# The first stage of a decoder layer: the first two weight blocks multiplied side by side, slice by slice

## The reference, cut to what matters

```python
mod = jax.nn.silu(c) @ w_ada + b_ada
sh1, sc1, gt1, sh2, sc2, gt2 = jnp.split(mod[:, None, :], 6, axis=-1)
u = x * (1 + sc1) + sh1
proj = u @ w_in
xa, ga, q, k, v = jnp.split(proj, [D_A, 2 * D_A, ...], axis=-1)
y_a, new_conv, h_last = rglru_branch(xa, ga, ...)
```

## Time and profile before

| | us |
|---|---|
| median of three runs | 1359.38 |
| lowest and highest of them | 1357.69, 1365.87 |
| span of the profiled execution, first to last instruction | 1363.8 |
| PE busy in it | 1196.5 (88%) |
| ACT busy, DVE busy | 577.3, 735.4 |

### The profile page before, as it was taken

How to read it: one execution, slowest core, us unless ns; L and a number is a source line. 1 busy time by engine, 2 the same in 40 slices (tenths; PEclk the granted TensorE clock), 3 DMA queues, 4 the chain that set the end, 5 groups by cost and what they waited for, 6 DMA issues and landing times. The chain is left out here.

```text
span 1363.8 us, 20897 instructions
## 1 busy us (share of the span) xinstructions
PE 1196.5 (88%) x6933; PEld 907.3 (67%) x6934; DVE 735.4 (54%) x1247; ACT 577.3 (42%) x845; POOL 137.3 (10%) x129
## 2 busy tenths in 40 slices
PE   5699899999699979969995389999999999999854
PEld 3699787877255647627783277777778877778721
DVE  3356534343356747527545775789641455476147
ACT  2556443111245644214233264677531454465124
POOL 0000000000000001002431200011000000000055
PEclk8799899999699999879997599999999999999977
DMA  9985931259669948877333596899661455597184
GB/s 333 368 289 195 354 126 64 70 179 333 242 206 352 307 134 273 272 208 233 126 119 130 183 335 261 324 380 399 232 234 62 138 215 210 214 371 268 38 342 178
DMA packets 102028, 316.94 MB, mean 232 GB/s; under 512 B 12845, under 2 KB 21533, under 8 KB 95290
## 3 DMA queue, kind: packets, MB, share of 16 engines
q1 hardware_dynamic: 85146, 273.97, 57.5%
q0 software_dynamic: 6432, 23.33, 4.8%
q10 hardware_dynamic: 10384, 18.76, 3.7%
HBM read 281.22 MB, written 101.93 MB: 281 GB/s over the span
## 5 line engine op out<-in xcount | busy, mean ns | idle before, releaser
L2584 DVE TENSOR_TENSOR e_downl<-e_wd,e_downh 128x1024 fp32r<-128x1024 f32 x64 | 74.1, 1220 | 65.3 <-ACT e_downh L2479 65.3
L2646 PE MATMUL e_psY<-e_downh,e_hTh 128*128 128x512 f32 x216 | 91.0, 421 | 15.7 <-DVE e_hTl L2605 14.5
L2479 ACT CAST e_downh<-e_wd 128x1024 fp32r<-128x1024 f32 x64 | 62.4, 1048 | 68.5 <-DMA e_wd<-in_w_exp_down 68.5
L552 PE MATMUL n_psA<-n_wh,u_h 128*128 128x512 f32 (+1 forms) x216 | 88.1, 408 | 0.4 <-DVE n_wl L811 0.4
L2646 PE MATMUL e_psG<-e_gateh,e_xTh 128*128 128x512 f32 x216 | 86.4, 400 | 2.0 <-DVE e_gatel L2578 2.0
L2646 PE MATMUL e_psG<-e_uph,e_xTh 128*128 128x512 f32 x216 | 87.8, 406 | 0.2 <-issue 0.2
L2648 PE MATMUL e_psG<-e_gatel,e_xTh 128*128 128x512 f32 x216 | 85.9, 398 | 0.0
L2647 PE MATMUL e_psG<-e_gateh,e_xTl 128*128 128x512 f32 x216 | 85.9, 398 | 0.0
L554 PE MATMUL n_psA<-n_wh,u_l 128*128 128x512 f32 (+1 forms) x216 | 85.8, 397 | 0.0
L2647 PE MATMUL e_psY<-e_downh,e_hTl 128*128 128x512 f32 x216 | 85.7, 397 | 0.0
L2648 PE MATMUL e_psY<-e_downl,e_hTh 128*128 128x512 f32 x216 | 85.5, 396 | 0.0
(11 more groups left out here) (406 smaller groups left out, 2573.0 us busy)
## 6 DMA issues: line engine op xcount, KB each, us to landing
e_wg<-in_w_exp_gate SPq DMA_DIRECT2D x16, 2048.0 KB
e_wu<-in_w_exp_up SPq DMA_DIRECT2D x16, 2048.0 KB
e_wd<-in_w_exp_down SPq DMA_DIRECT2D x16, 2048.0 KB, 14.4
out_k_s<-in_cache_win_k SPq DMA_DIRECT2D x8, 4088.0 KB, 21.1
out_v_s<-in_cache_win_v SPq DMA_DIRECT2D x8, 4088.0 KB, 34.5
a_wring<-in_w_ada SPq DMA_DIRECT2D x16, 1024.0 KB, 5.3
scratch_y<-e_y ACTq DMA_DIRECT2D x54, 256.0 KB, 4.3
n_wr<-in_w_in SPq DMA_DIRECT2D x20, 512.0 KB, 7.0
```

Of the source, the lines that this page charges most:

```text
L552: nc.tensor.matmul(dst, lh, rh, start=(k == 0), stop=False)
L2479: nc.scalar.copy(w["down"][H_][:, k, :], ew["down"][:, k, :]).then_inc(s_dh.sem, s_dh.unit)
L2584: nc.vector.tensor_tensor(w["down"][L_][:, k, :], ew["down"][:, k, :], w["down"][H_][:, k, :], ALU.subtract).then_inc(s_dl.sem, s_dl.unit)
L2646: nc.tensor.matmul(dst, left[H_], right[H_], start=first, stop=False)
```

## The change

SP issues the bias and the last three slices of `w_ada` of half 0 ahead of pieces 0 and 1. On PE, `branch` loses its range of k, and a new function `first_branches(k, halves)` multiplies slice k with X0 and with G0 one after the other; G0 takes the pair with the lower u second and that with the lower weight last. It waits for the upper and lower parts separately, ahead of each group of three matmuls. The eight slices of modulation half 1 are spread: four before the products of k = 0, and the rest between the products of k = 0, 1 and 2. `turn_mod(1)` follows k = 2. On ACT the order becomes `scaled(k)`, `upper_u(k)` for each k, with the cast of piece 1 after k = 0. On DVE `lower(0)` moves behind the modulation of the sample tokens and `lower(1)` behind `lower_u(0)`. In the ACT and DVE loops the condition k == 0 holds in half 0 only.

```diff
--- before.py
+++ after.py
@@ -388,15 +388,15 @@
             for k in range(3, 5):
                 load_ada(0, k)
             load_x(NT)
-            load_piece(0)
-            load_piece(1)
-            for k in range(5, KD):
-                load_ada(0, k)
             sp.wait_ge(s_z.sem, s_z.at(5))
             for j in range(QUAD):
                 x, b = divmod(j, 2)
                 src = b_ada[:, x * D:(x + 1) * D].rearrange("o (h b m) -> o h b m", h=2, b=2)[:, :, b, :]
                 sp.dma_start(bias[QROWS * j:QROWS * j + NSEQ, :, :], src.to_broadcast([NSEQ, 2, HALF])).then_inc(s_bias.sem, s_bias.unit)
+            for k in range(5, KD):
+                load_ada(0, k)
+            load_piece(0)
+            load_piece(1)
             for k in range(KD):
                 load_ada(1, k)
             r = 0
@@ -490,22 +490,36 @@
                     pe.wait_ge(s_xv.sem, s_xv.at(NTT))
                     pe.wait_ge(s_xe.sem, s_xe.at(NTT))
 
-            def branch(name, ks=range(KD)):
+            def branch(name):
                 n, e = BLOCKS.index(name), event[name]
                 r = n % RING
                 h, l = (w[:, r, :].rearrange("p (k m) -> p k m", k=KD) for w in (wh, wl))
-                if ks[0] == 0:
-                    bank_free(e)
-                    pe.wait_ge(s_wl.sem, s_wl.at(n + 1))
-                for k in ks:
-                    if e < 2:
-                        pe.wait_ge(s_ul.sem, s_ul.at(k + 1))
+                bank_free(e)
+                pe.wait_ge(s_wl.sem, s_wl.at(n + 1))
+                for k in range(KD):
                     for left, right in ((h, uh), (l, uh), (h, ul)):
                         for j in range(3):
                             last = nc.tensor.matmul(psA[:, 3 * (e % 2) + j, 0:CH], left[:, k, :], right[:, k, j * CH:(j + 1) * CH],
                                                     start=(k == 0 and left is h and right is uh), stop=(k == KD - 1 and right is ul))
-                if ks[-1] == KD - 1:
-                    last.then_inc(s_pe.sem, s_pe.unit)
+                last.then_inc(s_pe.sem, s_pe.unit)
+
+            def first_branches(k, halves="XG"):
+                for half in halves:
+                    n = e = "XG".index(half)
+                    h, l = (w[:, n, :].rearrange("p (k m) -> p k m", k=KD) for w in (wh, wl))
+                    if k == 0:
+                        bank_free(e)
+                    for i, (left, right) in enumerate(((h, uh), (l, uh), (h, ul)) if half == "X" else ((h, uh), (h, ul), (l, uh))):
+                        if k == 0:
+                            s = s_wl if left is l else s_wh
+                            pe.wait_ge(s.sem, s.at(n + 1))
+                        s = s_ul if right is ul else s_uh
+                        pe.wait_ge(s.sem, s.at(k + 1))
+                        for j in range(3):
+                            last = nc.tensor.matmul(psA[:, 3 * e + j, 0:CH], left[:, k, :], right[:, k, j * CH:(j + 1) * CH],
+                                                    start=(k == 0 and i == 0), stop=(k == KD - 1 and i == 2))
+                    if k == KD - 1:
+                        last.then_inc(s_pe.sem, s_pe.unit)
 
             def gate(name):
                 c, e = int(name[1]), event[name]
@@ -586,15 +600,21 @@
             for k in range(5, KD):
                 modulate(0, k)
             turn_mod(0)
-            low, high = range(KD // 2), range(KD // 2, KD)
-            branch("X0", low)
-            for k in range(KD):
+            for k in range(4):
                 modulate(1, k)
-            branch("G0", low)
+            first_branches(0)
+            modulate(1, 4)
+            first_branches(1)
+            modulate(1, 5)
+            modulate(1, 6)
+            first_branches(2, "X")
+            modulate(1, 7)
+            first_branches(2, "G")
             turn_mod(1)
-            branch("X0", high)
+            first_branches(3)
             constants_rows()
-            branch("G0", high)
+            for k in range(KD // 2, KD):
+                first_branches(k)
             for name in EARLY[2:]:
                 (branch if name[0] in "XG" else gate)(name)
                 if name in ("G2", "G3"):
@@ -731,15 +751,14 @@
             for t in range(NTT):
                 turned_x(t)
             upper(0)
-            upper(1)
             act.wait_ge(s_xv.sem, s_xv.at(NTT))
             for h in range(2):
                 act.wait_ge(s_ms.sem, s_ms.at(h + 1))
-                scaled(4 * h)
                 for k in range(4 * h, 4 * h + 4):
-                    if k % 4 < 3:
-                        scaled(k + 1)
+                    scaled(k)
                     upper_u(k)
+                    if k == 0:
+                        upper(1)
             upper(2)
             upper(3)
             act.wait_ge(s_co.sem, s_co.at(1))
@@ -925,8 +944,6 @@
             nc.vector.tensor_copy(silu[:, :, :], cT[:, :, 0:NSEQ]).then_inc(s_cT.sem, s_cT.unit)
             for t in range(NTT):
                 turned_x(t)
-            lower(0)
-            lower(1)
             v.wait_ge(s_bias.sem, s_bias.at(QUAD))
             v.wait_ge(s_xe.sem, s_xe.at(NTT))
             v.wait_ge(s_xv.sem, s_xv.at(NTT))
@@ -945,8 +962,12 @@
                 per = lambda i: modS[:, i, ks, 1:NSEQ].unsqueeze(3).to_broadcast([P, KD // 2, B, TS])
                 st.link(nc.vector.tensor_tensor(xq, xq, per(1), ALU.mult))
                 nc.vector.tensor_tensor(xq, xq, per(0), ALU.add).then_inc(s_us.sem, s_us.unit)
+                if h == 0:
+                    lower(0)
                 for k in range(4 * h, 4 * h + 4):
                     lower_u(k)
+                    if k == 0:
+                        lower(1)
             lower(2)
             lower(3)
             constant_columns()
```

## The result

| | before | changed |
|---|---|---|
| median of six runs each, us | 1361.55 | 1350.1 |
| lowest, highest | 1357.69, 1365.87 | 1348.45, 1352.26 |
| profiled execution: span (its time) | 1363.8 | 1349.7 (1351.48) |
| X1 starts, us | 78.38 | 67.43 |

The ratio is 0.993, with a 95% interval of 0.9905 to 0.9956: the changed kernel is faster by 0.4 to 1.0%, and 1350.1 us stands beside a forecast of 1349.4. In the runs of the experiments the execution's time is 1.75 to 2.03 us above its span. The two spans therefore differ by 14.1 us where the medians differ by 11.5.

A forecast was written before the change was run, and what follows sets the result against it. PE, busy 88% of 1363.8 us, was taken as the bound, with two 10.3 us waits each followed by a slow start. X1 10.0 us earlier made 1359.4 - 10.0 = 1349.4 us, range 1344.5 to 1355.5.

The forecast's parts named there:

- the sum: Whole kernel: X1 starts 10.0 us earlier, at 68.35 instead of 78.38, and the median falls to 1349.4 us.
- Loads: SP's queue: pieces 0 and 1 behind half 0's last slices bring these 3.5 us net, bounds 3.0 and 4.7.
- PE's new start: Start of X0: PE waits 3.4 us for half 1's fourth slice; first product at 38.5, 1.1 us sooner.
- The clock: PE's first products: the clock rises at 42.8 us, with 15 product matmuls slow until then.
- early-clock rival: Products of k = 0: earlier modulation bursts raise the clock, 2.0 us more gain, 1346.7 to 1347.4; chance 0.27.
- To the turn: Products and four modulation slices after k = 0 take 7.7 us; half 1's turn at 51.7 instead of 57.74.
- ACT, DVE and the tail: Turn to X1: ACT starts at 52.45, X0's eviction ends at 68.2, a new 1.0 us wait, X1 at 68.35.
- More waits: PE's 54 waits instead of 18 in this stage cost 0; 36 exposed reads would leave 6.4 to 8.2 us.
- Slower, the clock stays low: Rival, 38.5 us to X1: mixed products and modulations stay at the lower clock, X1 8.6 us later, 1368.0; chance 0.05.
- After X1: Everything behind X1, including the DMA chain at 151 us, shifts too while the gain is under about 17 us.
- "given back" rival: ACT or PE meets something late (piece 3, X1's chain, exposed waits): 2 to 6 us lost, 1351.5 to 1355.5; chance 0.20.

The follow-up runs named there:

- e1: PE's new order alone, with SP's loads and the ACT and DVE programs of the kernel before; median 1351.07 us, ratio 0.9932 against the kernel before.
- e3: The kernel before with one move: turn_mod(1) after the first slice of G0 instead of its fourth; median 1352.98 us, ratio 0.9941.
- e4: The changed kernel with all eight slices of modulation half 1 ahead of the products, turn after k = 0; 1355.84 us, ratio 0.9952 against before.
- e8: Changed kernel with products after one slice of modulation half 1, X0 finished ahead of G0, squares after the third v tile; 1344.97 us, ratio 0.9916 against before.
- e9: The kernel before with 22 matmuls that nobody reads in PE's gap ahead of X0's second half; one run, 1359.41 us beside 1357.99.
- e7: e1 with X0 finished two slices ahead of G0 and the constant columns ahead of the lower weights; 1350.13 us, ratio 0.9935 against before.
- e5: The changed kernel once more, unchanged, with a new profile; median 1349.5 us, ratio 0.9945 against the kernel before.
- e11: The kernel before with ACT scaling and then casting each slice instead of scaling one slice ahead; one run, 1359.20 us beside 1357.99.

## Why the prediction was right

The gain at X1 was 10.95 us where the sum had 10.0, and its terms hold nearly one by one.

- *Loads.* The last slice of half 0 is multiplied at 27.70 and not 28.5: the two pieces were worth 4.3 us, nearer the row's 4.7 than the 3.5 taken. The spacing of the `w_ada` slices was the wrong price for them.
- *PE's new start.* PE did wait for the fourth slice of half 1, and the first product came at 37.71 (38.5 forecast), 0.8 us sooner because the slice landed sooner (with the old loads, in e1, it was multiplied at 37.52 and not 36.70, so the assumption that it lands as before was off by this much). u was ready at 32.9 (34.0 forecast), and e1 shows how little it mattered here.
- *The clock.* It rose at about 41.4 us, 3.7 us after the first product. Before it had risen at about 45.4 (by the 0.94 of the earlier trace rows from 45.0 on), 5.7 us after the first product at 39.65. There were 12 slow matmuls, not 15. So a part of the early-clock rival came true. e1 shows that rival whole: modulation in one run raised the clock before any product.
- *To the turn.* 50.92 against 51.7. From the first product to the turn it is 13.21 us where the sum had 13.2: the three slow matmuls fewer (0.4 us) were used up by slower steps elsewhere, so this agreement is in part luck. e3 and e4 confirm where the gain was put: the turn moved ahead of work that covers its chain (5.8 us alone), and products while slices land (some 3).
- *ACT, DVE and the tail.* ACT restarts 0.75 us behind the turn as computed, the eviction is at 66.35 (67.2), the new wait is 0.86 (1.0), X1 at 67.43 (68.35).
- *More waits.* Zero was right. From 57.70 to 60.62 us in the changed kernel 18 matmuls with six waits take 2.92 us, as 18 times 0.162 do. By the price in the Trainium skill (Advanced Engine Details and Errata, Miscellaneous Facts, Network/Comms), fully exposed, the gain would have been 6.4 to 8.2 us. That did not come out: here, with matmuls queued, no such read shows.
- *Slower, the clock stays low.* False from 43 us on (1.00, products and modulations mixed). The Trainium skill's warning (TensorE: Matmul & The Clock Gate, Loop structure matters more than you think) fits the stretch up to 38 us, where each slice waits for its DMA at 0.50, and e4 up to 43 us. The page draws it with a long wait ahead of every matmul; here the waits between slices are 0.27 to 0.28 us. This nest leaves it once the loads are in.
- *After X1.* The rigid shift holds to 141 us (10.8 of 10.95). It failed at the squares, in some executions: 3.7 us went there. I had read the stretch at 110 us and the one at 151 but not the place at 172 where ACT and DVE, who hang on a recurrence, and PE meet. In the profile before, PE came late enough because it ran at the low clock twice ahead of it, after its wait of 5.47 us for the eviction of 152.1 and again inside the first v tile. It was a loss of the size of my "given back" rival, but not at one of the places I had named, and not in every run.

The total agrees better than the steps deserve. The forecast of 1349.4 rests on a gain 0.95 us too small, a give-back that I did not see, a median before of 1359.4 that became 1361.55 with three more runs, and executions of one kernel that spread over 13 us; the median's interval allows a gain of 6.0 to 12.9 us.

What stays open: why PE's gap near 140 us is 4.00 us in one execution of the changed kernel and 5.09 in the next, why the clock falls near 160 us in one with PE busy and not in the other, and how often each comes. The gap ends with a piece of weights that stands behind cache copies, and no kernel took those away. The profiles pair the short gap with the later wait, e3 excepted; no run set the gap or the clock there. That e1 and the changed kernel are equal in time is likely, not shown (intervals 0.9895 to 0.9969 and 0.9905 to 0.9956). In e8 the share of the tail and of the squares in the 1345 us was not separated from that of the early products.

## What to carry to other kernels

Price a wait by what it covers: when a small step (here a turn of two matmuls) starts a long chain on other engines, put it ahead of independent work that is as long as the chain, before rebuilding anything larger. An earlier load is worth only what its consumer's queue lets through: look at which wait stands directly ahead of the first use, and move load and order together. Follow a gain to the next place where engines that did not speed up meet the one that did, and read more than one execution there before calling the shift rigid.

## What the runs showed of the hardware

- The first product was followed by a different time at the low clock: about 5.7 us before, 4.2 in e3 (which has the same code up to there), 4.9 in e4, 3.7 in the changed kernel, and none in e1, where 24 small modulation matmuls in one run had come first. So one code's slow start differs by 1.5 us from execution to execution.
- Matmuls that nobody reads kept the clock up over a gap of 5 us (e9: 0.75 us for three products behind it, against 1.25).
- A single wait of 2.56 us at full clock was followed by 8 us at 0.57 to 0.58. After a gap of 4.00 us near 140 the restart was at full clock, after one of 5.09 at 0.50, in two executions of one kernel. A shorter gap did not spare it: after 3.01 us in e7 six matmuls took 3.73 us, where the restart at full clock had 2.53.
- The clock also fell with PE busy: in e5 from about 160.3 to 163.6 us (0.57 from 160 to 164), and in three other profiles at the same place. The last thing ahead of it was a run of 18 matmuls of one column (1.99 us). In the nine other profiles the same run was not followed by a fall there. No run tells why.
- Scaling one slice ahead of the cast cost the first slice of each half 1.0 us (e11). It brought the last slice only 0.6 us sooner: a slice came every 2.11 us with it and every 2.25 without.
